# Sample tile of a hybrid streaming encoder: state decays as whole-head products, head norms in row form, a reordered prologue, and w_out's first two blocks in two halves

## What is computed

```python
def even_mixer(xn, ...):            # cut to what the change touches
    qkv_a, z_a, beta_a, a_a, q_b, k_b, v_b, o_b, i_b, f_b = split(xn @ w_in)
    o_a, S = gated_delta_chunked(q_a, k_a, v_a, beta, g, S0)   # 4 heads, S' = exp(gL) S + k_end^T u
    o_a = o_a * rsqrt(mean(o_a^2) + EPS) * gdn_norm_w * silu(z_a)
    h_b, C, n, m = mlstm_chunked(q_b, k_b, v_b, logi, logf, C0, n0, m0)  # 4 heads, C' = decay C + kw^T v
    h_b = h_b * rsqrt(mean(h_b^2) + EPS) * mlstm_norm_w * sigmoid(o_b)
    return concat([o_a, h_b]) @ w_out, states
```

## Time and profile before

| | |
|---|---|
| three runs | 2781.73, 2781.47, 2777.7 us; median 2781.47 |
| the profiled execution | 2778.89 us, span 2777.0 us |
| mean granted clock of TensorE | 0.979 of full |
| busy | PE 2682.8 us (97%), weight loads 2637.6 (95%), DVE 1870.2 (67%), ACT 1080.3 (39%), POOL 522.1 (19%) |
| chain that ended last | PE 82%, DVE 14%, ACT 2% |

### The profile page before, as it was taken

One profiled execution on the slowest core, in us unless ns is written; L12 is line 12 of the kernel. 1 busy time (PEld: TensorE's weight loads), 2 busy tenths in 40 slices (PEclk: granted clock), 3 DMA queues, 4 the chain that ended last, 5 costly groups with the idle time before them and its releaser, 6 DMA issues.

```text
span 2777.0 us, 43628 instructions
## 1 busy us (share of the span) xinstructions
PE 2682.8 (97%) x18131; PEld 2637.6 (95%) x18131; DVE 1870.2 (67%) x2234; ACT 1080.3 (39%) x1588; POOL 522.1 (19%) x247
## 2 busy tenths in 40 slices
PE   6999999999998899999999899999999999999997
PEld 6999999999998789999999899999999999999997
DVE  7748476987677468657476883856666786584755
ACT  5525254233223435435244452533421254252544
POOL 3020303232010011110203203020233411102031
PEclk9999999999999779999999999999999999999998
DMA  3322323232003212323232223232222223232231
GB/s 104 91 71 82 92 73 88 54 79 54 16 9 76 70 47 77 92 70 91 69 95 65 64 77 91 77 91 73 80 84 76 71 67 98 65 95 72 85 87 46
DMA packets 401245, 205.56 MB, mean 74 GB/s; under 512 B 15651, under 2 KB 399036, under 8 KB 401049
## 3 DMA queue, kind: packets, MB, share of 16 engines
q1 hardware_dynamic: 400842, 202.70, 25.7%
q10 hardware_dynamic: 206, 0.08, 0.0%
HBM read 195.14 MB, written 7.60 MB: 73 GB/s over the span
## 4 chain that ended last, share of the span: by engine, by line
PE 82%; DVE 14%; ACT 2%; issue 1%; POOL 0%; DMA 0%; ACTq 0%; DVEq 0%
PE ps L866 12%; PE ps L880 12%; PE ps L867 12%; PE ps L870 12%; PE ps L882 12%; PE ps L881 12%; PE ps L955 3%; PE ps L981 1%; PE ps L1085 1%; DVE ct L2512 1%; DVE r L2053 1%; DVE ct L2509 1%; DVE hf L2366 1%; DVE ut L1945 1%; PE ps L949 1%
## 5 line engine op out<-in xcount | busy, mean ns | idle before, releaser
L820 POOL TENSOR_TENSOR wlo<-raw,whi 128x1024 fp32r<-128x1024 f32 (+2 forms) x210 | 510.4, 2434 | 2209.5 <-ACT whi L1464 2209.5
L866 PE MATMUL ps<-xh,whi 128*128 128x320 f32 x1488 | 455.2, 314 | 22.6 <-POOL wlo L820 6.5
L867 PE MATMUL ps<-xl,whi 128*128 128x320 f32 x1488 | 450.3, 310 | 0.0
L866 PE MATMUL ps<-hh,whi 128*128 128x320 f32 x1440 | 437.9, 312 | 11.5 <-DVE hl L2030 4.4
L867 PE MATMUL ps<-hl,whi 128*128 128x320 f32 x1440 | 434.7, 310 | 0.0
L880 PE MATMUL ps<-tau_hi,whi 128*128 128x320 f32 x1328 | 412.6, 311 | 3.9 <-DVE wlo L1961 2.0
L882 PE MATMUL ps<-tau_hi,wlo 128*128 128x320 f32 x1328 | 411.5, 310 | 0.0
L881 PE MATMUL ps<-tau_lo,whi 128*128 128x320 f32 x1328 | 411.5, 310 | 0.0
L1464 ACT CAST whi<-raw 128x1024 fp32r<-128x1024 f32 (+2 forms) x210 | 202.6, 965 | 394.1 <-PE ps L870 352.5
L870 PE MATMUL ps<-xh,wlo 128*128 128x320 f32 x1488 | 340.8, 310 | 0.0
L870 PE MATMUL ps<-hh,wlo 128*128 128x320 f32 x1440 | 329.1, 310 | 0.0
(11 more groups left out here) (386 smaller groups left out, 4973.1 us busy)
## 6 DMA issues: line engine op xcount, KB each, us to landing
raw<-in_ffn_w_gu SPq DMA_DIRECT2D x332, 256.0 KB, 3.8
raw<-in_ffn_w_d SPq DMA_DIRECT2D x64, 512.0 KB, 4.0
raw<-in_w_in_even SPq DMA_DIRECT2D x32, 512.0 KB, 4.1
raw<-in_ffn_w_d SPq DMA_DIRECT2D x32, 384.0 KB, 3.5
raw<-in_w_in_odd SPq DMA_DIRECT2D x24, 512.0 KB, 3.7
raw<-in_w_ple_gate SPq DMA_DIRECT2D x16, 512.0 KB, 3.9
raw<-in_ffn_w_gu SPq DMA_DIRECT2D x10, 512.0 KB, 4.5
raw<-in_w_out_even SPq DMA_DIRECT2D x8, 512.0 KB, 4.5
```

What stands on the lines that cost most here:

```text
L820: pool.tensor_tensor(ring(wlo, n), raw[:, slot, 0:kt, :], ring(whi, n).bitcast(fp32), ALU.subtract).then_inc(lo_ready, 1)
L866: pe.matmul(ps[j % 4][:, c, 0:HT], wh[:, k], hi[:, k, cs], start=(k == 0), stop=False)
L867: pe.matmul(ps[j % 4][:, c, 0:HT], wh[:, k], lo[:, k, cs], start=False, stop=False)
```

## The change

- **Prologue**: DVE's copy of prompt tile 3's output goes to ACT, which is idle there. "up1" moves from the middle of `delta_head` to its end. The mLSTM parts lie one level later; DVE forms both k and q products right after level 2, and the qk and q steps of mLSTM after level 3. "kend" comes before "vt"; "vt" comes after the read of S. The gates are activated ahead of the read, one instruction of 640 tokens for each head where there were two.
- **Between read and u**: the transposes and u come before the second numerator; o comes before the first `state_c`.
- **Decays**: `decay_s` and `decay_c` multiply a head's 8 states by their decays in one product of 1024 columns; S decays follow the read, C decays follow that head's numerator (new semaphore `num_done`). What is left after the state product is an addition in two instructions of 512 columns. The first spread of u is one product on DVE (`u_first`) in place of eight copies on ACT.
- **Norms in row form**: squares are the moving operand and a 24-column picker (`pick`, one column of ones) the stationary one, so that sums of four heads accumulate in 24 rows of 128 tokens. The root is one instruction, and the inverse one of 24 x 128. `o_spread` has the rows as its moving operand, 24 rows in all six products. Norms 0 to 3 are spread and applied between the state updates; heads 4 to 7 follow.
- **w_out**: "pad" jobs, which are only counted and freed, shift its PSUM tiles so that the first block lies in `ps[3]` and the second in `ps[0]`. Block 0 runs its steps 0 to 3 as soon as heads 0 to 3 are ready, then the last two norms are spread, then come steps 0 to 3 of block 1, steps 4 to 7 of block 0 and steps 4 to 7 of block 1.

```diff
         def norm_chunks(q, c):
-            k = q % HA * 2 + c
-            base = 24 * (q // HA)
-            return [(0, P, base + 2 * k), (P, P, base + 2 * k + 1), (2 * P, HT - 2 * P, base + 16 + k)]
+            k = (q % HA * 2 + c) * 3
+            return [(0, P, k), (2 * P, HT - 2 * P, k + 2), (P, P, k + 1)]
...
             def o_sums(first):
...
+                for i, (q, c, (off, w, row)) in enumerate(steps):
+                    last = pe.matmul(bank(1 - first // HA)[0:6 * HA, 0:w], pick[:, 6 * HA - 1 - row:12 * HA - 1 - row],
+                                     o_squares(q)[:, c, off:off + w], start=(i == 0), stop=(i == len(steps) - 1), skip_group_check=True)
...
                 for c in range(2):
-                    for off, w, col in norm_chunks(q, c):
-                        last = pe.matmul(out[:, c, off:off + w], ncol[0:w, col:col + 1].to_broadcast([w, P]), ident[0:w, 0:w],
+                    for off, w, row in norm_chunks(q, c):
+                        last = pe.matmul(out[:, c, off:off + w], ident[0:6 * HA, row:row + 1].to_broadcast([6 * HA, P]), rrow[:, q // HA, 0:w],
...
+                per_head(4, lambda h: W(7)[:, h], lambda h: W(8)[:, h]).then_inc(core["u"], 1)
                 sample_part("kt")
                 sample_num(1)
 
-                pe.wait_ge(core["rtok"], t + 1)
-                per_head(4, lambda h: W(7)[:, h], lambda h: W(8)[:, h]).then_inc(core["u"], 1)
+                pe.wait_ge(core["utok"], t + 1)
+                per_head(0, lambda h: W(1)[:, h], lambda h: W(5)[:, h]).then_inc(core["o"], 1)
                 state_c(0)
                 sample_num(2)
-
-                pe.wait_ge(core["utok"], t + 1)
-                per_head(0, lambda h: W(1)[:, h], lambda h: W(5)[:, h]).then_inc(core["o"], 1)
+                sample_num(3)
+                sample_part("den")
                 state_c(1)
-                sample_num(3).then_inc(ms_pe, 1)
-                sample_part("den")
                 sample_part("nsum")
+                o_sums(0)
                 state_s(0)
-                o_sums(0)
                 state_c(2)
+                o_spread(0)
                 state_s(1)
+                o_spread(1)
                 state_c(3)
+                o_spread(2)
+                o_sums(HA)
                 state_s(2)
-                o_sums(HA)
+                o_spread(3)
                 state_s(3)
-                for q_ in range(2 * HA):
-                    o_spread(q_, ps[(3, 0)[q_ % 2]])
...
                 last.then_inc(n_moved, 1)
+                o_spread(4)
+                o_spread(5)
+
+            def first_blocks(s):
...
+                pe.wait_ge(o_used, HA)
+                mm(n, hi, lo, first=(h_ready, s["hbase"]), part=(0, HA))
+                o_spread(6)
+                o_spread(7)
+
+                pe.wait_ge(states_done, 2)
+                mm(n + 1, hi, lo, part=(0, HA))
+                mm(n, hi, lo, first=(h_ready, s["hbase"]), part=(HA, KD))
+                mm(n + 1, hi, lo, part=(HA, KD))
...
+                def decay_c(h):
+
+                    dve.wait_ge(num_done, h + 1)
+                    mul(stc[:, h, :, 0:P], stc[:, h, :, 0:P], last_of(VS(1)[:, h]))
+
                 def add_c(h):
 
                     dve.wait_ge(c_product, h + 1)
-                    for b in range(DECB):
...
+                    for c in range(2):
+                        sm = c_added if c else dve_own
+                        own(dve.tensor_tensor(stc[:, h, 4 * c:4 * c + 4, 0:P], stc[:, h, 4 * c:4 * c + 4, 0:P],
+                                              ps[1][:, c, :].rearrange("p (b v) -> p b v", v=P), ALU.add).then_inc(sm, 1), sm)
...
+                for h in range(HA):
+                    decay_s(h)
+                decay_c(0)
+                decay_c(1)
...
+                inverse(0)
                 add_s(0)
+                normalise(0)
                 add_c(2)
+                normalise(1)
                 add_s(1)
+                normalise(2)
                 add_c(3)
+                normalise(3)
                 add_s(2)
+                low(0)
+                low(1)
                 add_s(3)
...
+                inverse(1)
+                low(2)
+                low(3)
+                for q_ in range(HA, 2 * HA):
+                    normalise(q_)
+                for q_ in range(HA, 2 * HA):
+                    low(q_)
```

More of the change, by code:

```diff
@@ L448, in stream_step @@
             blk((w_in, (wcol[3] if q < HA else bcol[3]) + q % HA * P), KD, "z")
-        stages.append(dict(kind="down", n0=len(blocks), kt=KD, last=True, scale=1.0, hbase=pairs, prod=prod, g=2 * KD, tau=ntau, stored=16, hid=other(prod - 1)))
+        stages[-1]["pads"] = [job("pad") for _ in range((3 - len(jobs)) % 4)]
+        stages.append(dict(kind="down", n0=len(blocks), kt=KD, last=True, scale=1.0, hbase=pairs, prod=prod, g=2 * KD, tau=ntau, stored=16, split=True, hid=other(prod - 1)))
         for o in range(KD):
@@ L1368, in _ @@
                 elif kind == "down":
-                    for o in range(KD):
+                    if s.get("split"):
+                        first_blocks(s)
+                    for o in range(2 if s.get("split") else 0, KD):
                         mm(s["n0"] + o, *s["hid"], first=(h_ready, s["hbase"]) if o == 0 else None)
@@ new lines, in _ @@
+                    act.activation(VS(2), heads(7), ACT.Exp).then_inc(ms_act, 1)
+                    act.wait_ge(ms_pe, MS_PE.index("kend") + 1)
+                    act.activation(VS(4), heads(7), ACT.Exp).then_inc(ms_act, 1)
+                    for q in range(2 * HA):
+                        if q % HA == 0:
+                            act.wait_ge(z_scaled, 4 * (NTILE - 1) if q else 10)
+                        act.activation(z_both(q), z_both(q), ACT.Silu if q < HA else ACT.Sigmoid).then_inc(z_act, 1)
@@ L2086, in delta_head @@
                 mul(v, v, heads(0))
-                if t:
+                sample = t == NTILE - 1
+                if t and not sample:
                     o1(dve.tensor_copy(qkv[:, 16:16 + HA, (t - 1) * P:t * P], heads(2)))
@@ new lines, in sample_tile @@
+                own(dve.tensor_tensor(spread_u(0), W(1)[:, 0].unsqueeze(1).to_broadcast([P, DECB, P]),
+                                      bmask[:].unsqueeze(2).to_broadcast([P, DECB, P]), ALU.mult).then_inc(u_first, 1), u_first)
+                decay_c(2)
+                decay_c(3)
+                dve.wait_ge(ms_act, MS_ACT.index("den") + 1)
+                o1(dve.tensor_tensor(VS(0), VS(0), VS(2), ALU.max))
+                o1(dve.reciprocal(VS(0), VS(0)))
+                own(dve.tensor_tensor(bv, heads(7), VS(0), ALU.mult).then_inc(o_new, 1), o_new)
```

230 lines of the change are left out of this document (113 added, 117 removed).

## The result

Four executions of the changed kernel took 2758.4, 2761.67, 2762.07 and 2762.76 us, median 2761.87; the kernel before, run beside it, had a median of 2780.1 (2777.7 to 2781.73, four). The ratio is 0.9926 (0.9913 to 0.9939): 18.2 us, faster by 0.7%. The profiled execution took 2758.4 us, span 2756.7, against 2777.0 of the span before: 20.3 us, where the sum of the forecast says 20.5. The mark that I follow, the start of the second add on x, went from 1015.78 to 995.98: 19.8 us. Of these, 1.76 were there before the stage began: the last update of the prompt's S starts at 870.76 in this trace and at 872.52 in the trace before. Where kernels are compared by stage, times count from the entry.

A forecast was written before the change was run, and what follows sets the result against it. Sample tile bound by busy but half-clocked PE and a serial end; gap -26.3, blocks +3, sections before +3 gave 20.5 us off, 2758.4 from 2778.89 or 2761.0 from the median: forecast 2760, own range 2753 to 2765, 8 in 10 2751 to 2771.

The forecast's parts named there:

- Prologue: Before the read of S: level 1 starts 1.2 us earlier, the read only 0.7, at 897.1 for 897.8.
- Read to o: From the read of S, at half clock from 901, to DVE seeing o at 922.3, 3.4 us earlier than 925.65.
- Prices: Assumed instruction costs: PE record 0.11 us at full clock, 0.21 at half; spread 1.35 or 2.6; sums 4.5; inverse 0.9.
- the other bound: Dearer price for spreading one head's norm: today's pace, 3.5 us at half clock; the forecast took the cheaper.
- The rival of bare weight loads: Spreads and sums cost more because every record's weight load lies bare: +8 to +10 us, 2769; chance 0.09.
- Decays: DVE's state updates: add_c 1.45 us for 3.03, 2.7 with decay; eight heads fall only 3 us, step between products halves.
- The new wait: After S3, DVE's low(0) and low(1) wait for ACT's hi copies, delaying add_s(3) to 969.9 and the inverse to 970.8.
- o to the last update: State updates with norms 0 to 3 between them: last add ends 969.9 (before 966.9), section 3 us later.
- Tail: Last update to block 1's end: gap shrinks by 26.3 us, both blocks 16.3 become 19.3, end seen at 995.3.
- The clock: PE idle at 957.7 to 961.2 and 965.8 to 970.9: half clock from the first until the dense blocks.
- The rival with half clock between 921 and 957: Half clock in part of that stretch, numerators 2 and 3 standing together: +8 to +12 us, 2769; chance 0.11.
- gap 32.5 becomes 6.2: Time in us between the last state update and the start of w_out block 0: a gain of 26.3.

The follow-up runs named there:

- batch 1: Changed kernel again 2760.07 us; against it: old prologue 2765.47, first two w_out blocks unsplit 2763.17, decays back in the add 2773.48.
- batch 2: Kernel before with row-form norms alone 2766.43 us; changed kernel without the new wait 2755.11, that with old prologue 2755.85, or with numerators apart 2756.34.
- batch 3: Kernel before with row-form norms and whole-head decays 2758.96 us; changed kernel without wait, spreads ahead 2751.48, plus wider products 2749.09; changed with wider products 2760.0.

## Why the prediction was right, and where it wasn't

The forecast of 2760 lies 2 us from the median, and the sum of 20.5 us agrees with 20.3 in the span. Part of this agreement is luck. Of the 20.3 us, 1.8 were there before the stage began, so the stage itself gave 18.0 of the 20.5. Within it a late read and a read quicker than forecast cancel, and the second profile of the same kernel gives 11.2 us for the stage (143.3 to 132.1). By its steps:

- **Prologue: wrong.** I had the read start 0.7 us earlier. From the entry it came 28.6 us later, where the kernel before has 25.3, and thus 4 us after the forecast. Two things failed. PE waits 2.14 us for DVE's "gates" (the first line of its timeline above), where the old order waits 0.87; I had seen this wait and priced it too low. And PE was at half clock for 13.7 us between the entry and the read, where the trace before has 3.4; the sum has nothing for that. In the other profiles of the new prologue (6.8 to 10.2 us at half clock) the read starts 26.6 to 28.3 us after the entry, in those of the old one (3.4 to 6.8 us) 25.2 to 26.5: it was never early. SP's loads of S, moved to 882.6 (I said 883.5), were in time: the read doesn't wait for them. In seven later profiles of the new prologue DVE does wait 1.7 to 2.6 us for the n states, one of my signs of being wrong, but it is done with them before the read ends.
- **Read to o: right.** o at DVE 921.3, forecast 922.3, but with 3.2 us less than I gave it from the read (21.95 for 25.2), since 901 to 921.5 was at 0.67 and not at 0.50. The read itself was 2.2 us later than forecast (899.3 for 897.1), so the two errors cancel but for 1 us. That is luck.
- **Prices: right but one.** Products of 1024 columns 1.25, adds 1.41 a pair, sums 4.57 (4.5), inverse 0.94 (0.9). A spread took 1.60 at full clock for my 1.35 and 2.74 at half for 2.6. The 3.5 of the other bound was at half clock and lies well above the 2.74. The rival of bare weight loads would have given 2.7 us or more at full clock: it fell. (Its own sum is off: one more load of 0.11 to 0.21 for each of 12 records is 1.3 to 2.5 us, not 1.3 to 2.) The Trainium skill (TensorE: Matmul & The Clock Gate, "What overlaps and what doesn't") would have that rival come; 0.13 us for each record of 24 rows, all in the same rows, contradicts it as the sets of four did.
- **Decays: right in size, wrong in weight.** "DVE's work on the eight heads falls by only 3 us, but the step between two products halves" holds; I didn't price what the halved step is worth. At the mark it is 7.9 us in the new order (13.4 in the medians, at unlike clocks) and 5.0 in the old one (6 in the ratios, 0.9942 to 0.992). Eight instructions of 128 columns take 3.03 us and one of 1024 takes 1.25 for the same elements, though the eight also add and read PSUM; for one operation, 512 columns take 0.69 and 1024 take 1.22 to 1.25, less than twice. The Trainium skill (VectorE: DVE Perf Modes, "The TRN2 errata — SBUF-src ops pay a fixed extra latency per instruction") has a fixed cost for each instruction; these rows agree.
- **The new wait: right in place and size.** Low 0 and 1 forecast to end at 968.4, measured 966.8; the inverse at 970.8, measured 969.2; the first spread after it follows at once. I took it as the price of the change. It was 5 us that moving a few lines brings back, and the prediction could have said that.
- **o to the last update: right.** The reciprocal ended at 933.2 (935.8), the second sums at 952.7 (954.6), the last add at 968.2 (969.9), 1.3 later than before. Counted from the entry it ended 3.0 later, the 3 of the forecast.
- **Tail: the gap right, the blocks too cheap.** Forecast start of the first half block 976.0, measured 974.65, so the gap behind the last add is 6.4 us for 6.2. The second add on x was forecast near 995.3 and measured at 995.98: the two blocks took 21.3 us for the 19.3 forecast. I had the clock at full from about 980; it was at half until 979.5 and again from about 983 to 986.5.
- **The clock.** Half clock from the gaps after 957.7, as forecast (0.72, then 0.55), and a rise within the blocks. The rival with half clock between 921 and 957 did come, in the second profile of the changed kernel (2766.14 us), one of two among six executions with a mean clock of 0.981; the other has no profile. I had given it 0.11, as if it were a property of the kernel. It is the same kernel in another execution, and my range of 2751 to 2771 holds both.
- **What the gain is made of: wrong.** I put all 26 us of the tail down to the new order with row norms. The runs say: norms in row form, left where they were, 15.7 us; the decays a further 6 (the intervals just touch, the executions don't); interleaving, split and prologue together nothing, as long as the new wait stands. The prediction never asked what each part is worth without the others, since its sum follows one schedule. The term "gap 32.5 becomes 6.2" is right as a reading and misleading as a cause: against the kernel with both parts in the old order, the last update ends 14 us later.

What stays open: how much of the gain is work and how much clock; why single executions of one kernel differ by 10 us in where the clock falls, and whether the old prologue makes the slower ones more frequent (its five executions in batch 1 all lie above 2763, four of six of the changed kernel lie below 2761; in batch 2 there is no such difference). The place of the numerators wasn't settled either.

## What to carry to other kernels

Change the shape of the instructions before their order: 24-row operands for the norms and one product of 1024 columns for eight decays gave all of the gain in the old order, while moving the same work between the updates gave nothing until the wait that it had made was gone (then 7.5 us, batch 3). When a queue is interleaved by hand, look in it for an instruction that waits for something young and stands ahead of one whose inputs are old (the low part ahead of the last add and the inverse: 5 us at like clock). And a sum that follows one schedule needs a second sum, for each part alone, before it is said where a gain comes from.

## What the runs showed of the hardware

- **PE wholly busy was granted half clock.** From 901.0 to 921.5 the kernel before is busy 20.5 of 20.5 us at 0.50, with products that move 32, 16 and 128 columns. With one product of 512 columns, of rounded numbers, ahead of every four of those with 32 or 16 the same window had 1.00 in the one profile of each of the two kernels tried, busy 19.26. The Trainium skill (TensorE: Matmul & The Clock Gate, "Why this matters for your kernels") puts a fall down to idle gaps between bursts; the trace agrees after 959, and contradicts it as the only cause in the read.
- **The same program differs by 10 us between executions**, and the clock goes with it: mean granted clock 0.984 at 2756.7 and 0.981 at 2767.3; in its two profiles, 13.6 us more at half clock and a mark 6.8 us later. For a change of 20 us this asks for several executions of each kernel, and for the windows of each profile, before two of them are set side by side.
